# A three-pass float32r linear layer: steady weight tiles over four token blocks (256, 256, 256, 288) instead of three blocks of 352

## The chip, the cores and the metric

The kernel runs on one core of one Trainium2 chip. The metric is the device time of one launch in microseconds (us): the median of three runs before the change. Everything below comes from the reference, the kernel's text, these run times and the trace of one profiled execution.

## What is computed

One inference step of a two-layer trunk of width 1024. 1024 prompt tokens and 32 sample tokens (8 sequences of 4) share all weights, so each linear layer sees 1056 tokens. Layer 0 mixes tokens by a gated short convolution, layer 1 by stick-breaking attention; each is followed by a convolutional FFN of inner width 2816.

```python
h = rmsnorm(x, norm_mix[i])
if i % N_MIXERS == 0:                      # layer 0
    proj = h @ w_in                        # 1024 -> 3 * 1024
    b_gate, c_gate, v = split(proj, 3)
    y = (b_gate * causal_dwconv(c_gate * v, prev, w_dw)) @ w_out
else:                                      # layer 1
    qkv = h @ w_qkv
    y = stick_breaking(q, k, v, ...) @ w_o
x = x + y
h = rmsnorm(x, norm_ffn[i])
up = h @ w_up                              # 1024 -> 2 * 2816
g, u = split(up, 2)
a = silu(causal_dwconv(g, prev, w_dw) + b_dw) * u
x = x + a @ w_down                         # 2816 -> 1024
```

## The kernel before

**Numbers.** Activations and weights are float32. Each is split in two float32r parts, `hi` and `lo`, and a product is made of three passes of TensorE: `w_hi*hi`, `w_hi*lo` and `w_lo*hi`, all added up in PSUM. The helper `three` issues the three matmuls of one block; each has its own load of 128x128 weights in front. float32r and float32 both stand as "f32" in the rows of PE.

**Tiles.** All weights are cut into 196 tiles of 128x1024 (24 for `sc_in`, 8 for `sc_out`, 66 for each FFN, 24 for `qkv`, 8 for `wo`). A tile is brought in by a DMA into `raw`, split by POOL (w_hi L506, w_lo L508), and used 8 times 128 columns. Tokens are the moving side: 1056 = 3 blocks of TW = 352 columns, so a weight block of 128x128 gives 3 blocks x 3 passes = 9 matmuls, and a tile 72; 196 tiles give 14112.

**PSUM.** `out[0]` and `out[1]` have three banks of 512 float32 each. A block of 352 tokens stands at the start of each bank; `result(s)` is the view 128x3x352 over them. The two are used in turn: PE waits for `taken[s]`, fills, and raises `full[s]`; DVE (or ACT) then reads all 1056 columns in one instruction and raises `taken[s]`.

**Places.** `linear` (a whole tile, contraction over k inside) and `down` (the FFN's second product: two tiles are summed into each of 8 outputs) are the steady code. The first tile of a stage (`first_linear`, which waits for its input block by block), the last (`last_linear`), the last `down` of an FFN (`last_down`) and the attention's `project` work block by block with other semaphores. PE's program is written out in full and its order is that of the code; nothing is scheduled at run time.

**Readers of PSUM named below.** `ffn_chunk` (L1463 and L1474), `add_x` (L1486), the short convolution (L1525), and ACT's `copy_gate` (L958).

Of the kernel before, what the change touches and what calls it, by code (L numbers as in the profile page):

```python
# [27 lines left out]
T = SEQ + NS  # L28
TJ = 3
TW = T // TJ  # L30
F = 2816
FC = F // P
CW = 3
# [143 lines left out]
def build(nc, x_in, weights, taps_sc, taps_ffn, state_sc, state_ffn, gains, bias_heads, bias_rows,  # L177
# [6 lines left out]
    with ctx:  # L184
# [103 lines left out]
        def result(s):  # L288
            return out[s][:, :, 0:TW]

        score = [out[1][:, 0:2, :].rearrange("p a b -> p (a b)"), spare[:, :, :].rearrange("p a b -> p (a b)")]
        def wide(t):
            return t.rearrange("p (a b) -> p a b", a=TJ)
# [4 lines left out]
        def tokens(j):  # L298
            return slice(j * TW, (j + 1) * TW)

# [237 lines left out]

        @block.tensor
        def _(pe):  # L540
            def three(o, w, c0, hi, lo, first, last, counts=False):

                mm = nc.tensor.matmul(o, w_hi[w][:, c0:c0 + P], hi, start=first, stop=False)  # L543
                if counts:
                    mm.then_inc(w_used, 1)
                nc.tensor.matmul(o, w_hi[w][:, c0:c0 + P], lo, start=False, stop=False)  # L546
                return nc.tensor.matmul(o, w_lo[w][:, c0:c0 + P], hi, start=False, stop=last)  # L547

            def mean_of(nth, j, n):

# [12 lines left out]
            def linear(tile, ring, s, fill, midway=None):  # L563

                pe.wait_ge(w_split, tile + (RAW + 1))

                pe.wait_ge(taken[s], fill + 1)
                for k in range(KC):
                    for j in range(TJ):

                        mm = three(out[s][:, j, 0:TW], ring, k * P, h_hi[:, k, tokens(j)],
                                   h_lo[:, k, tokens(j)], k == 0, k == KC - 1, k == j == 0)
                    if midway is not None:
                        midway(k)
                mm.then_inc(full[s], 1)
# [51 lines left out]
            def down(tile, ring0, k0, name, trip, slot, group, early_release):  # L627

                order = [(f, kk) for f in range(KC) for kk in range(2)]
                if early_release:  # L630


                    order[-4:] = [(KC - 2, 0), (KC - 1, 0), (KC - 2, 1), (KC - 1, 1)]
                release = (KC - 2, 1) if early_release else (KC - 1, 1)
                for f, kk in order:
                    s = (k0 + f + 1) % 2
                    if f == 0:

                        pe.wait_ge(w_split, tile + (RAW + 1 + kk))
                        pe.wait_ge(a_ready, group * 2 + (3 + kk))  # L640
                    if kk == 0:
                        pe.wait_ge(taken[s], trip * TRIP_FILLS + (FREE[name][s] + (k0 + f) // 2 + 1))
                    for j in range(TJ):

                        mm = three(out[s][:, j, 0:TW], (ring0 + kk) % SPLIT, f * P,
                                   a_hi[:, slot, kk, j * TW:(j + 1) * TW],
                                   a_lo[:, slot, kk, j * TW:(j + 1) * TW], kk == 0, kk == 1,
                                   j == 0 and (f, kk) in (order[0], release))
                    if kk == 1:
                        mm.then_inc(full[s], 1)  # L650

# [304 lines left out]
        def _(act):  # L956
# [36 lines left out]
            def copy_gate(m):  # L993
                n, k = m % 2, 3 * m
                s = (k + 1) % 2
                act.wait_ge(convolved, m + 1)
                act.wait_ge(full[s], FULL["sc_in"][s] + k // 2 + 1)
                act_op(wide(c_gate[n][:, :]), result(s)).then_inc(taken[s], 1)

            def first_norm():  # L1000
                act.preload_act_table(ACT.Sqrt)
# [325 lines left out]
        def _(dve):  # L1327
# [52 lines left out]

            def norm_of_projection(nth, name, base):
                for f in range(KC - 1):
                    add_x(f, name, f, 0)
                    n = SUM_BASE[nth] + f
                    dve.wait_ge(squared, SQ_BASE[nth] + f + 1)
                    if f == 0:
                        V.tensor_copy(total[:, :], square[0][:, :]).then_inc(summed, 1)
                    else:
                        dve.wait_ge(summed, n)
                        V.tensor_tensor(total[:, :], total[:, :], square[f % 2][:, :], ALU.add).then_inc(summed, 1)  # L1390
                f, added = KC - 1, TJ * (nth // 2)
                s = (f + 1) % 2
                for j in range(TJ):
                    dve.wait_ge(block_full, base + j + 1)
                    V.tensor_tensor(x[:, f, tokens(j)], x[:, f, tokens(j)], out[s][:, j, 0:TW], ALU.add).then_inc(x_added, 1)
                    for g in range(KC):
                        low(nth, g, j)
                for j in range(TJ):
                    sum_block(nth, f, j, f + j)
                dve.wait_ge(x_added, added + TJ)  # L1400
                dve.sem_inc(taken[s], 1)
                invert_all(nth)
# [51 lines left out]
                        last.then_inc(tapped, 1)  # L1454
                last.then_inc(convolved, 1)

            def ffn_chunk(m, par, chunk, layer, k, trip, slot, between=None):
                name = f"ffn{layer}"
                s = (k + 1) % 2

                dve.wait_ge(convolved, m + 1)
                dve.wait_ge(full[s], trip * TRIP_FILLS + (FULL[name][s] + k // 2 + 1))
                V.tensor_tensor(wide(ext[par][:, CW - 1:]), result(s), wide(rstd[:, :]), ALU.mult).then_inc(taken[s], 1)  # L1463
                dve.wait_ge(taken[s], trip * TRIP_FILLS + (FREE[name][s] + k // 2 + 2))

                dve.wait_ge(a_ready, m - (KC - 1))
                conv(m, par, lambda t: tap_ffn[:, ds(chunk + layer * FC, 1), t:t + 1].rearrange("p o t -> p (o t)"))
                s = (k + 2) % 2
                dve.wait_ge(silued, m - (KC - 1))
                V.tensor_tensor(y[par][:, :], y[par][:, :], rstd[:, :], ALU.mult).then_inc(y_scaled, 1)  # L1470
                dve.wait_ge(y_scaled, m + 1)
                dve.wait_ge(full[s], trip * TRIP_FILLS + (FULL[name][s] + (k + 1) // 2 + 1))
                yy = wide(y[par][:, :])
                V.tensor_tensor(yy, yy, result(s), ALU.mult).then_inc(taken[s], 1)  # L1474
                if between is not None:
                    between()
                dve.wait_ge(a_high, m - (KC - 1))
                V.tensor_tensor(a_lo[:, slot, par, :], y[par][:, :], a_hi[:, slot, par, :].bitcast(f32),
                                ALU.subtract).then_inc(a_ready, 1)

            def add_x(f, name, k, trip):

                s = (k + 1) % 2
                dve.wait_ge(full[s], trip * TRIP_FILLS + (FULL[name][s] + k // 2 + 1))
                xx = x[:, f, :].rearrange("p (a b) -> p a b", a=TJ)
                V.tensor_tensor(xx, xx, result(s), ALU.add).then_inc(taken[s], 1)  # L1486

            def ffn(layer):
                name = f"ffn{layer}"
                m0 = M_FFN[layer]  # L1490

                def up(m, chunk, k0, trip, slot, between=None):
                    for p in range(2):
                        ffn_chunk(m + p, p, chunk + p, layer, k0 + 2 * p, trip, slot, between if p else None)

                def down(k0, trip):
                    for f in range(1, KC):
                        add_x(f, name, k0 + f, trip)

                up(m0, 0, 0, 0, 0)  # L1500
                with dve.Fori(0, FFN_TRIPS) as i:
                    for n in range(2):
                        k0 = (4 + KC) * n + 4
                        up(i * 4 + (m0 + 2 + 2 * n), i * 4 + (2 + 2 * n), k0, i, (n + 1) % 2,
                           lambda: add_x(0, name, k0 + 4, i))
                        down(k0 + 4, i)
# [7 lines left out]
            def sc_in_chunk(i, n, last=False):  # L1514
# [7 lines left out]
                V.tensor_tensor(c_gate[n][:, :], c_gate[n][:, :], rstd2[:, :], ALU.mult).then_inc(c_scaled, 1)  # L1522
                dve.wait_ge(c_scaled, m + 1)
                dve.wait_ge(full[s], i * 3 + (FULL["sc_in"][s] + k // 2 + 1))
                V.tensor_tensor(wide(ext[n][:, CW - 1:]), wide(c_gate[n][:, :]), result(s), ALU.mult).then_inc(taken[s], 1)  # L1525
                dve.wait_ge(taken[s], i * 3 + (FREE["sc_in"][s] + k // 2 + 2))
                conv(m, n, lambda t: tap_sc[:, ds(m, 1), t:t + 1].rearrange("p o t -> p (o t)"))

# [12 lines left out]
                    dve.sem_inc(taken[s], 1)  # L1541
                else:
                    dve.wait_ge(full[s], i * 3 + (FULL["sc_in"][s] + k // 2 + 1))
                    V.tensor_tensor(mixed[:, ds(m, 1), :].rearrange("p o (a b) -> p (o a) b", a=TJ),
                                    wide(y[n][:, :]), result(s), ALU.mult).then_inc(taken[s], 1)

            with dve.Fori(0, KC // 2 - 1) as i:
                for n in range(2):
# [250 lines left out]
```

## Time and profile before

| | |
|---|---|
| Runs | 2622.76 us median of 3 (2622.29 to 2626.1) |
| Profiled execution, first to last instruction (span) | 2615.1 us |
| PE (matmul) busy | 2570.0 us, 98% |
| PE weight load busy | 2443.8 us, 93% |
| DVE, ACT, POOL busy | 1374.5, 550.8, 708.4 us |
| Mean granted TensorE clock | 0.996 |

The profile gives the span of the profiled execution, and no other time of it; the median of the runs lies 7.7 us above that span, which is what lies around it. Busy time of PE counts each matmul from its start to its last result, and neighbours overlap, so a busy share near 100% says that PE hardly waits, and the distance from one start to the next says what a matmul costs.

### The profile page before, as it was taken

How to read it: one execution, taken by the hardware profiler on the slowest of the kernel's cores; microseconds unless marked ns; L12 is line 12 of the kernel's file. 1: busy time of each engine (PE TensorE's matmuls, PEld its weight loads, DVE VectorE, ACT ScalarE, POOL GpSimd, SP SyncE). 2: the span in 40 equal slices, each digit the busy share in tenths (PEclk: the TensorE clock that was granted, in tenths of full speed). 3: DMA queues.
4: the chain of work that ended last, by engine and by line, in shares of the span. 5: the costliest groups of instructions: out<-in, count | busy, mean ns of one | idle time of the engine just before them, and what ended most of it. 6: DMA issues, size and time to landing. Idle time of an engine off the chain costs nothing.

```text
span 2615.1 us, 40858 instructions
## 1 busy us (share of the span) xinstructions
PE 2570.0 (98%) x16982; PEld 2443.8 (93%) x16982; DVE 1374.5 (53%) x1346; ACT 550.8 (21%) x1145; POOL 708.4 (27%) x405
## 2 busy tenths in 40 slices
PE   8999999999999999999999999999999999999997
PEld 7999999999999999988888888669999999999996
DVE  5333446444544444476667666654644455444445
ACT  4000221000000000144444444542100000000012
POOL 3333333323322333322111111013332332233331
PEclk9999999999999999999999999999999999999999
DMA  4111111111111111122111111641111111111111
GB/s 142 43 47 49 47 44 49 41 49 48 42 41 49 49 49 49 44 70 95 35 40 36 39 42 42 211 172 41 49 41 49 49 41 41 49 49 49 49 44 67
DMA packets 62523, 149.06 MB, mean 57 GB/s; under 512 B 5666, under 2 KB 28962, under 8 KB 62370
## 3 DMA queue, kind: packets, MB, share of 16 engines
q1 hardware_dynamic: 56130, 130.35, 15.6%
q10 hardware_dynamic: 6240, 16.36, 1.6%
q8 instruction: 134, 2.20, 0.4%
q14 instruction: 19, 0.16, 0.0%
HBM read 128.91 MB, written 17.78 MB: 56 GB/s over the span
## 4 chain that ended last, share of the span: by engine, by line
PE 92%; DVE 5%; issue 2%; ACT 1%; POOL 1%; DMA 0%; DVEq 0%; POOLq 0%; ACTq 0%; SPq 0%
PE bank L543 28%; PE bank L547 28%; PE bank L546 27%; PE bank L807 2%; PE bank L745 2%; DVE prod L1591 2%; PE bank L778 2%; DVE beta L1595 1%; PE bank L680 0%; PE bank L748 0%; DVE h_lo L1432 0%; DVE rstd L1366 0%; PE bank L881 0%; PE bank L912 0%; POOL w_lo L521 0%
## 5 line engine op out<-in xcount | busy, mean ns | idle before, releaser
L543 PE MATMUL bank<-h_hi,w_hi 128*128 128x352 f32 x3648 | 1189.0, 326 | 14.4 <-DVE h_lo L1352 7.6
L547 PE MATMUL bank<-h_hi,w_lo 128*128 128x352 f32 x3648 | 1175.2, 322 | 0.0
L546 PE MATMUL bank<-h_lo,w_hi 128*128 128x352 f32 x3648 | 1171.6, 321 | 0.0
L506 POOL CAST w_hi<-raw 128x1024 fp32r<-128x1024 f32 x194 | 212.5, 1095 | 1841.9 <-PE bank L543 1795.2
L543 PEld LDWEIGHTS bank<-h_hi,w_hi 128*128 128x128 f32 x3648 | 685.0, 188 | 24.2 <-issue 14.8
L546 PEld LDWEIGHTS bank<-h_lo,w_hi 128*128 128x128 f32 x3648 | 689.0, 189 | 0.8
L547 PEld LDWEIGHTS bank<-h_hi,w_lo 128*128 128x128 f32 x3648 | 685.1, 188 | 0.0
L508 POOL TENSOR_TENSOR w_lo<-raw,w_hi 128x1024 fp32r<-128x1024 f32 x194 | 478.4, 2466 | 15.5
L1486 DVE TENSOR_TENSOR x<-x,bank 128x1056 f32<-128x1056 f32 x174 | 218.3, 1254 | 320.5 <-PE bank L547 318.6
L543 PE MATMUL bank<-a_hi,w_hi 128*128 128x352 f32 x1056 | 343.7, 325 | 2.3 <-POOL w_lo L508 2.3
L546 PE MATMUL bank<-a_lo,w_hi 128*128 128x352 f32 x1056 | 340.8, 323 | 0.0
L547 PE MATMUL bank<-a_hi,w_lo 128*128 128x352 f32 x1056 | 340.7, 323 | 0.0
L1591 DVE TENSOR_TENSOR_SCAN prod<-keep 128x895 f32<-128x895 f32 (+7 forms) x128 | 216.6, 1692 | 86.9 <-ACT keep L958 80.0
L1463 DVE TENSOR_TENSOR ext<-bank,rstd 128x1056 f32<-128x1056 f32 x44 | 55.4, 1258 | 339.9 <-PE bank L547 339.8
L958 ACT ACTIVATE smp<-ext 128x32 f32<-128x32 f32 x52 | 12.0, 231 | 939.1 <-DVE ext L1463 850.9
L543 PEld LDWEIGHTS bank<-a_hi,w_hi 128*128 128x128 f32 x1056 | 198.4, 188 | 10.3 <-DVE x L1407 3.4
L546 PEld LDWEIGHTS bank<-a_lo,w_hi 128*128 128x128 f32 x1056 | 198.5, 188 | 0.3
L547 PEld LDWEIGHTS bank<-a_hi,w_lo 128*128 128x128 f32 x1056 | 198.4, 188 | 0.0
L1438 DVE TENSOR_SCALAR y<-ext,tap_ffn 128x1024 f32<-128x1024 f32 x44 | 116.5, 2649 | 9.7 <-DVE ext L1463 9.6
L958 ACT ACTIVATE beta<-bank,bias_pair 128x896 f32<-128x896 f32 (+7 forms) x128 | 94.9, 742 | 126.0 <-PE bank L748 120.7
L1445 DVE SCALAR_TENSOR_TENSOR y<-ext,tap_ffn,y 128x1024 f32<-128x1024 f32 x88 | 113.0, 1284 | 0.0
L1595 DVE TENSOR_TENSOR beta<-beta,prod 128x895 f32<-128x895 f32 (+7 forms) x128 | 106.2, 829 | 4.4
(129 smaller groups left out, 1622.3 us busy)
## 6 DMA issues: line engine op xcount, KB each, us to landing
raw<-weights SPq DMA_DIRECT2D x196, 512.0 KB, 3.5
x_spill<-x ACTq DMA_DIRECT2D x8, 528.0 KB, 5.1
k_out<-k_t ACTq DMA_DIRECT2D x8, 528.0 KB, 3.1
v_out<-v_t ACTq DMA_DIRECT2D x8, 528.0 KB, 2.7
x<-x_spill SPq DMA_DIRECT2D x8, 528.0 KB, 7.3
pages_hi<-cache_k SPq DMA_DIRECT2D x8, 512.0 KB, 6.0
pages_hi<-cache_v SPq DMA_DIRECT2D x8, 512.0 KB, 7.2
pages_lo<-cache_k SPq DMA_DIRECT2D x8, 512.0 KB, 7.4
```

The source lines that it names most:

```text
L506: nc.gpsimd.tensor_copy(w_hi[ring][:, :], raw[slot][:, :]).then_inc(w_high, 1)
L508: nc.gpsimd.tensor_tensor(w_lo[ring][:, :], raw[slot][:, :], w_hi[ring][:, :].bitcast(f32), ALU.subtract).then_inc(w_split, 1)
L543: mm = nc.tensor.matmul(o, w_hi[w][:, c0:c0 + P], hi, start=first, stop=False)
L546: nc.tensor.matmul(o, w_hi[w][:, c0:c0 + P], lo, start=False, stop=False)
L547: return nc.tensor.matmul(o, w_lo[w][:, c0:c0 + P], hi, start=False, stop=last)
L958: return nc.scalar.activation(o, i, func, **kw)
L1438: V.tensor_scalar(o[:, 0:SEQ], e[:, 0:SEQ], tap(0), None, ALU.mult).then_inc(tapped, 1)
L1445: main = V.scalar_tensor_tensor(o[:, 0:SEQ], e[:, n:n + SEQ], tap(n), o[:, 0:SEQ], ALU.mult, ALU.add)
L1463: V.tensor_tensor(wide(ext[par][:, CW - 1:]), result(s), wide(rstd[:, :]), ALU.mult).then_inc(taken[s], 1)
L1486: V.tensor_tensor(xx, xx, result(s), ALU.add).then_inc(taken[s], 1)
L1591: V.tensor_tensor_scan(prod[:, width - 1:0:-1], back, back, 1.0, ALU.mult, ALU.bypass).then_inc(scanned, 1)
L1595: V.tensor_tensor(w[:, 0:width - 1], w[:, 0:width - 1], prod[:, 1:width], ALU.mult).then_inc(weighed, 1)
```

## The change

In `linear` and `down` the 1056 tokens are cut at 256, 512 and 768. The output is no longer one block per bank: it stands contiguous from column 256 of the first bank to column 288 of the third (`flat(s)`), so that the first block fills the upper half of bank 0, the second and third fill bank 1, and the fourth, of 288, starts bank 2. Only the first block in each bank has the flag that clears (`CLEARS`). Readers of these tiles take one contiguous run of 1056 columns instead of three of 352. Tiles of `first_linear`, `last_linear`, `last_down` and `project` keep 352, and their readers keep `result(s)` (`by_blocks`).

```diff
+FLAT_AT = 256
+PARTS = ((0, 256), (256, 512), (512, 768), (768, T))
+CLEARS = (0, 256, 768)
+        def flat(s):
+            return out[s][:, :, :].rearrange("p a b -> p (a b)")[:, FLAT_AT:FLAT_AT + T]
...
                 for k in range(KC):
-                    for j in range(TJ):
-
-                        mm = three(out[s][:, j, 0:TW], ring, k * P, h_hi[:, k, tokens(j)],
-                                   h_lo[:, k, tokens(j)], k == 0, k == KC - 1, k == j == 0)
+                    for a, b in PARTS:
+
+                        mm = three(flat(s)[:, a:b], ring, k * P, h_hi[:, k, a:b], h_lo[:, k, a:b],
+                                   k == 0 and a in CLEARS, k == KC - 1, k == a == 0, True)
...
-                    for j in range(TJ):
-
-                        mm = three(out[s][:, j, 0:TW], (ring0 + kk) % SPLIT, f * P,
-                                   a_hi[:, slot, kk, j * TW:(j + 1) * TW],
-                                   a_lo[:, slot, kk, j * TW:(j + 1) * TW], kk == 0, kk == 1,
-                                   j == 0 and (f, kk) in (order[0], release))
+                    for a, b in PARTS:
+
+                        mm = three(flat(s)[:, a:b], (ring0 + kk) % SPLIT, f * P, a_hi[:, slot, kk, a:b],
+                                   a_lo[:, slot, kk, a:b], kk == 0 and a in CLEARS, kk == 1,
+                                   a == 0 and (f, kk) in (order[0], release), True)
...
+                if by_blocks:
+                    V.tensor_tensor(wide(ext[par][:, CW - 1:]), result(s), wide(rstd[:, :]), ALU.mult).then_inc(taken[s], 1)
+                else:
+                    V.tensor_tensor(ext[par][:, CW - 1:], flat(s), rstd[:, :], ALU.mult).then_inc(taken[s], 1)
```

On PE, at the start of the second tile of the program (a `linear` of the short convolution's input), one 128x128 block of weights is this before the change (`w_hi_55` and `w_lo_58` are the two parts of the tile):

```order
L543 MATMUL bank<-h_hi,w_hi_55 128x352
L546 MATMUL bank<-h_lo,w_hi_55 128x352
L547 MATMUL bank<-h_hi,w_lo_58 128x352
L543 MATMUL bank<-h_hi,w_hi_55 128x352
L546 MATMUL bank<-h_lo,w_hi_55 128x352
L547 MATMUL bank<-h_hi,w_lo_58 128x352
L543 MATMUL bank<-h_hi,w_hi_55 128x352
L546 MATMUL bank<-h_lo,w_hi_55 128x352
L547 MATMUL bank<-h_hi,w_lo_58 128x352
```

and this in the changed kernel:

```order
L552 MATMUL bank<-h_hi,w_hi_55 128x256
L555 MATMUL bank<-h_lo,w_hi_55 128x256
L556 MATMUL bank<-h_hi,w_lo_58 128x256
L552 MATMUL bank<-h_hi,w_hi_55 128x256
L555 MATMUL bank<-h_lo,w_hi_55 128x256
L556 MATMUL bank<-h_hi,w_lo_58 128x256
L552 MATMUL bank<-h_hi,w_hi_55 128x256
L555 MATMUL bank<-h_lo,w_hi_55 128x256
L556 MATMUL bank<-h_hi,w_lo_58 128x256
L552 MATMUL bank<-h_hi,w_hi_55 128x288
L555 MATMUL bank<-h_lo,w_hi_55 128x288
L556 MATMUL bank<-h_hi,w_lo_58 128x288
```

Nine matmuls became twelve, over the same 3 x 1056 columns. The whole program of PE has 11520 matmuls of 352 columns fewer, 11520 of 256 and 3840 of 288 more, and 2592 of its three-pass matmuls stay at 352. The other place is where the last `linear` of an FFN trip ends and `down` begins (`a_hi`, `a_lo` are the activated inner values). In the changed kernel, with the semaphores that the row waits for:

```order
L552 MATMUL bank<-h_hi,w_hi_54 128x288
L555 MATMUL bank<-h_lo,w_hi_54 128x288
L556 MATMUL bank<-h_hi,w_lo_57 128x288
L552 MATMUL bank<-a_hi,w_hi_55 128x256 [waits taken1,a_ready,w_split]
L555 MATMUL bank<-a_lo,w_hi_55 128x256
```

Before the change the same five rows are of 352 columns, with the same waits at the same row. No instruction of DVE, ACT, POOL or SP is added or taken away; those that read PSUM have another access pattern of the same 1056 columns.

## Rows read from the trace of the kernel before

**Rows 1.** The page: busy time, slices, the chain by line, costliest groups.

```profile
PE 2570.0 (98%) x16982; PEld 2443.8 (93%) x16982; DVE 1374.5 (53%) x1346; ACT 550.8 (21%) x1145; POOL 708.4 (27%) x405
...
PEclk9999999999999999999999999999999999999999
...
PE bank L543 28%; PE bank L547 28%; PE bank L546 27%; PE bank L807 2%; PE bank L745 2%; DVE prod L1591 2%; PE bank L778 2%; DVE beta L1595 1%; PE bank L680 0%; PE bank L748 0%; DVE h_lo L1432 0%; DVE rstd L1366 0%; PE bank L881 0%; PE bank L912 0%; POOL w_lo L521 0%
...
L543 PE MATMUL bank<-h_hi,w_hi 128*128 128x352 f32 x3648 | 1189.0, 326 | 14.4 <-DVE h_lo L1352 7.6
```

**Rows 2.** PE in time order, steady tile: start us, us, instruction.

```profile
1000.09 0.32 PE L543 MATMUL bank<-h_hi,w_hi 128*128 128x352 f32 x1
1000.25 0.32 PE L546 MATMUL bank<-h_lo,w_hi 128*128 128x352 f32 x1
...
1003.93 0.32 PE L543 MATMUL bank<-h_hi,w_hi 128*128 128x352 f32 x1
```

**Rows 3.** Windows: from:to length, busy (x count), then granted clock, DMA share, GB/s.

```profile
100.00:280.00 180.00, 180.00 (x1135) 180.00 (x1134) 56.03 (x51) 8.99 (x26) 61.01 (x32) 1.00 0.15 45
500.00:1000.00 500.00, 500.00 (x3113) 498.17 (x3112) 233.94 (x199) 40.83 (x98) 150.98 (x88) 1.00 0.15 47
```

**Rows 4.** Other forms on PE in time order, same columns as rows 2.

```profile
400.31 1.05 PE L552 MATMUL bank<-total,mean 128*128 128x352 f32 x3
...
1208.69 0.87 PE L778 MATMUL bank<-ident,beta 128*128 128x128 f32 x6
...
1208.69 1.09 PE L778 MATMUL bank<-ident,beta 128*128 128x128 f32 x8
...
1211.21 0.28 PE L748 MATMUL bank<-diag_b,ident_b 128*128 128x128 bf16 x2
1211.42 0.99 PE L807 MATMUL bank<-w_second,v_rows 128*64 128x128 f32 x14
```

**Rows 5.** By line: duration ns min/median/max of those forms.

```profile
L552 PE MATMUL bank<-total,mean x12: 456/458/460, 400.3 to 1844.0; 128*128 128x352 f32 x12
...
L748 PE MATMUL bank<-diag_b,ident_b x128: 218/224/231, 1192.2 to 1720.1; 128*128 128x128 bf16 x128
```

**Rows 6.** Weight loads by line; then in time order, after a stop and steady.

```profile
L680 PEld LDWEIGHTS bank<-square,mean x72: 105/107/110, 25.4 to 2598.2; 128*32 128x32 f32 x72
...
L552 PEld LDWEIGHTS bank<-total,mean x12: 187/189/189, 400.1 to 1843.7; 128*128 128x128 f32 x12
...
L778 PEld LDWEIGHTS bank<-ident,beta x576: 137/140/145, 1205.6 to 1727.3; 128*128 128x128 f32 x192
...
55.84 0.19 PEld L543 LDWEIGHTS bank<-h_hi,w_hi 128*128 128x128 f32 x1 [1.93 <-issue]
55.94 0.19 PEld L546 LDWEIGHTS bank<-h_lo,w_hi 128*128 128x128 f32 x1
...
1000.25 0.19 PEld L547 LDWEIGHTS bank<-h_hi,w_lo 128*128 128x128 f32 x1
```

**Rows 7.** PE waits, longest first: us in total, times, longest us.

```profile
PE bank L543 <- DVE h_lo L1352: 7.6, 2, 7.4
...
PE bank L543 <- DVE ext L1525: 1.7, 1, 1.7
```

**Rows 8.** DVE by line and form: busy us, mean ns, idle before, releaser.

```profile
L1486 DVE TENSOR_TENSOR x<-x,bank 128x1056 f32<-128x1056 f32 x174 | 218.3, 1254 | 320.5 <-PE bank L547 318.6 <-DMA x<-x_spill 2.0
...
L1470 DVE TENSOR_TENSOR y<-y,rstd 128x1056 f32<-128x1056 f32 x44 | 57.3, 1303 | 55.1 <-ACT y L958 55.1
```

**Rows 9.** PE in time order, first steady stage.

```profile
150.01 0.32 PE L546 MATMUL bank<-h_lo,w_hi 128*128 128x352 f32 x1
150.16 0.32 PE L547 MATMUL bank<-h_hi,w_lo 128*128 128x352 f32 x1
...
150.48 0.32 PE L546 MATMUL bank<-h_lo,w_hi 128*128 128x352 f32 x1
150.65 0.32 PE L547 MATMUL bank<-h_hi,w_lo 128*128 128x352 f32 x1
```

More of the change, by code:

```diff
@@ L540, in _, with three @@
         def _(pe):
-            def three(o, w, c0, hi, lo, first, last, counts=False):
-                mm = nc.tensor.matmul(o, w_hi[w][:, c0:c0 + P], hi, start=first, stop=False)
+            def three(o, w, c0, hi, lo, first, last, counts=False, shared=False):
+                mm = nc.tensor.matmul(o, w_hi[w][:, c0:c0 + P], hi, start=first, stop=False, skip_group_check=shared)
                 if counts:
                     mm.then_inc(w_used, 1)
-                nc.tensor.matmul(o, w_hi[w][:, c0:c0 + P], lo, start=False, stop=False)
-                return nc.tensor.matmul(o, w_lo[w][:, c0:c0 + P], hi, start=False, stop=last)
+                nc.tensor.matmul(o, w_hi[w][:, c0:c0 + P], lo, start=False, stop=False, skip_group_check=shared)
+                return nc.tensor.matmul(o, w_lo[w][:, c0:c0 + P], hi, start=False, stop=last, skip_group_check=shared)
             def mean_of(nth, j, n):
@@ L997, in copy_gate @@
                 act.wait_ge(full[s], FULL["sc_in"][s] + k // 2 + 1)
-                act_op(wide(c_gate[n][:, :]), result(s)).then_inc(taken[s], 1)
+                if m == 0:
+                    act_op(wide(c_gate[n][:, :]), result(s)).then_inc(taken[s], 1)
+                else:
+                    act_op(c_gate[n][:, :], flat(s)).then_inc(taken[s], 1)
             def first_norm():
@@ L1382, in norm_of_projection @@
                 for f in range(KC - 1):
-                    add_x(f, name, f, 0)
+                    add_x(f, name, f, 0, f == 0)
                     n = SUM_BASE[nth] + f
@@ L1455, in conv, with ffn_chunk @@
                 last.then_inc(convolved, 1)
-            def ffn_chunk(m, par, chunk, layer, k, trip, slot, between=None):
+            def ffn_chunk(m, par, chunk, layer, k, trip, slot, between=None, by_blocks=False):
                 name = f"ffn{layer}"
@@ L1462, in ffn_chunk @@
                 dve.wait_ge(full[s], trip * TRIP_FILLS + (FULL[name][s] + k // 2 + 1))
-                V.tensor_tensor(wide(ext[par][:, CW - 1:]), result(s), wide(rstd[:, :]), ALU.mult).then_inc(taken[s], 1)
+                if by_blocks:
+                    V.tensor_tensor(wide(ext[par][:, CW - 1:]), result(s), wide(rstd[:, :]), ALU.mult).then_inc(taken[s], 1)
+                else:
+                    V.tensor_tensor(ext[par][:, CW - 1:], flat(s), rstd[:, :], ALU.mult).then_inc(taken[s], 1)
                 dve.wait_ge(taken[s], trip * TRIP_FILLS + (FREE[name][s] + k // 2 + 2))
@@ L1472, in ffn_chunk @@
                 dve.wait_ge(full[s], trip * TRIP_FILLS + (FULL[name][s] + (k + 1) // 2 + 1))
-                yy = wide(y[par][:, :])
-                V.tensor_tensor(yy, yy, result(s), ALU.mult).then_inc(taken[s], 1)
+                V.tensor_tensor(y[par][:, :], y[par][:, :], flat(s), ALU.mult).then_inc(taken[s], 1)
                 if between is not None:
@@ L1479, in ffn_chunk, with add_x @@
                                 ALU.subtract).then_inc(a_ready, 1)
-            def add_x(f, name, k, trip):
+            def add_x(f, name, k, trip, by_blocks=False):
                 s = (k + 1) % 2
                 dve.wait_ge(full[s], trip * TRIP_FILLS + (FULL[name][s] + k // 2 + 1))
-                xx = x[:, f, :].rearrange("p (a b) -> p a b", a=TJ)
-                V.tensor_tensor(xx, xx, result(s), ALU.add).then_inc(taken[s], 1)
+                if by_blocks:
+                    V.tensor_tensor(wide(x[:, f, :]), wide(x[:, f, :]), result(s), ALU.add).then_inc(taken[s], 1)
+                else:
+                    V.tensor_tensor(x[:, f, :], x[:, f, :], flat(s), ALU.add).then_inc(taken[s], 1)
             def ffn(layer):
@@ L1490, in ffn, with up @@
                 m0 = M_FFN[layer]
-                def up(m, chunk, k0, trip, slot, between=None):
+                def up(m, chunk, k0, trip, slot, between=None, first=False):
                     for p in range(2):
-                        ffn_chunk(m + p, p, chunk + p, layer, k0 + 2 * p, trip, slot, between if p else None)
+                        ffn_chunk(m + p, p, chunk + p, layer, k0 + 2 * p, trip, slot, between if p else None, first and p == 0)
                 def down(k0, trip):
@@ L1498, in down @@
                         add_x(f, name, k0 + f, trip)
-                up(m0, 0, 0, 0, 0)
+                up(m0, 0, 0, 0, 0, first=True)
                 with dve.Fori(0, FFN_TRIPS) as i:
@@ L1524, in sc_in_chunk @@
                 dve.wait_ge(full[s], i * 3 + (FULL["sc_in"][s] + k // 2 + 1))
-                V.tensor_tensor(wide(ext[n][:, CW - 1:]), wide(c_gate[n][:, :]), result(s), ALU.mult).then_inc(taken[s], 1)
+                V.tensor_tensor(ext[n][:, CW - 1:], c_gate[n][:, :], flat(s), ALU.mult).then_inc(taken[s], 1)
                 dve.wait_ge(taken[s], i * 3 + (FREE["sc_in"][s] + k // 2 + 2))
@@ L1543, in sc_in_chunk @@
                     dve.wait_ge(full[s], i * 3 + (FULL["sc_in"][s] + k // 2 + 1))
-                    V.tensor_tensor(mixed[:, ds(m, 1), :].rearrange("p o (a b) -> p (o a) b", a=TJ),
-                                    wide(y[n][:, :]), result(s), ALU.mult).then_inc(taken[s], 1)
+                    V.tensor_tensor(mixed[:, ds(m, 1), :].rearrange("p o t -> p (o t)"),
+                                    y[n][:, :], flat(s), ALU.mult).then_inc(taken[s], 1)
             with dve.Fori(0, KC // 2 - 1) as i:
```

## Prediction

> **What bounds the kernel now.** I read the page first: PE is busy 98% of the span, the clock row is at its upper level (2.4 GHz) throughout, and in the chain that ended last the three lines of the three-pass product, L543, L546 and L547, hold 28 + 27 + 28 = 83% [rows 1]. So time is won or lost in how fast these matmuls follow each other. Next PE's waits: the longest single one is 7.4 us at the start, and no entry is of a steady tile that waits for its PSUM buffer for more than the single 1.7 us stop [rows 7]. PE streams.
>
> The busy time of one matmul, 326 ns [rows 1], is its whole way through the array, and neighbours overlap. What one costs is the distance of starts. In time order these are 0.16 us apart; 24 of them lie between the starts at 1000.09 and 1003.93, so 3.84 us / 24 = 160.0 ns each [rows 2]. Over long stretches, taking off the two in flight at the edge, it is 180/1133 = 158.9 ns while POOL and DVE are rather quiet and 500/3111 = 160.7 ns in the FFN [rows 3]. I take 160.0.
>
> At 2.4 GHz, 352 columns take 146.7 ns, so **a matmul costs 13.3 ns more than its columns** (12.2 to 14.0 by the two stretches). What this excess is made of decides the whole prediction, so I looked at what other forms have. Three float32 matmuls of 352 columns at L552 take 1.05 us, of which the last's own 0.458: 0.592/2 = 296 ns apart [rows 4, 5], which is 352 columns at half the rate (293.3) and 2.7. Transposes of 128 columns: eight end 0.22 us after six, 110 ns each [rows 4], that is 106.7 at half the rate and 3. Two bf16 matmuls at L748, at the full rate: 280 - 224 = 56 ns [rows 4, 5], 53.3 and 2.7. So every other form has an excess of about 3, and only float32r, 4 bytes per column at full rate, has 13. That it moves from place to place (starts 0.15 to 0.17 us apart in one stretch, [rows 9]) makes it look like the way operands are fetched.
>
> **The change, part by part.** (1) Matmuls. Of the 14112 three-pass matmuls 11520 lie in `linear` and `down`; they are 3840 groups of one pass over 1056 columns. Three become four, with the same columns. So the columns cost nothing more (1056/2.4 = 440.0 ns per group either way) and what changes is the excess: now 3 x 13.3 = 40 per group. If it is paid per matmul, the group goes from 480.0 to 440.0 + 4 x 13.3 = 493.3 ns, and 3840 x 13.3 = **+51.1 us**. With 12.2 and 14.0 for the excess: +47 and +54.
>
> Why per matmul: the three other forms, with 352 and 128 columns at either rate, all have the same 3 ns, so there the excess doesn't grow with the columns; and the variation of the float32r one by place is of a few ns per instruction. Why perhaps not: there is one width of float32r in this trace, and no row can separate a share per column from a share per matmul. That is the step I trust least.
>
> The Trainium skill (TensorE: Matmul & The Clock Gate, "Back-to-back issue gap") gives N/2.4 + 2.5 ns for warm matmuls. The rows of L552, L778 and L748 agree with it; the 160 ns of the float32r rows do not (it would give 149.2). By this rule an added matmul costs 2.5 ns and the change 3840 x 2.5 = +9.6 us; that is close to the second rival below.
>
> (2) Weight loads. Each added matmul has its own load, and all loads now have less to hide behind: 256 columns last 106.7 ns. A load of 32 columns shows 107 ns, one of 128 columns 189 [rows 6]: 82 ns for 96 columns, 0.85 ns each, so 109 ns of pure loading for 128. After a stop the second load starts 0.10 us after the first, when the first matmul begins [rows 6]: the same number. A load starts when the matmul before begins (both at 1000.25, [rows 2, 6]), so a block can't be shorter than about 110 ns; with the excess it is 120. I cost the loads at nothing. The cover shrinks from 50 ns to 10: if it fails, each nanosecond of a block costs 15.4 us over 15360 blocks. That is the third rival.
>
> (3) Reading instructions: 7680 more on PE, in pairs each 120 ns. In the attention 14 matmuls of L807 with their loads pass in 0.99 us [rows 4], less than 71 ns a pair. At nothing.
>
> (4) Readers of PSUM. DVE takes 1254 ns for 1056 columns out of three banks in three runs, and 1303 ns for 1056 contiguous ones in SBUF [rows 8]: no sign that three runs cost anything. Nobody waits for them either: a tile takes 72 x 160 = 11.5 us and an output of `down` 18 x 160 = 2.9 us, against 1.25 of DVE, which waited 318.6 us for PE there [rows 8]. If a reader were 0.1 us longer, it would still end before the other buffer is full. Below nothing: where PE stops for DVE's L1525 (1.7 us, once, [rows 7]) a faster reader gives back at most some tenths. At nothing.
>
> (5) Stages that keep 352 (2592 matmuls, the attention, the norms) are as before. POOL delivers w_hi and w_lo per tile as before, and has more time.
>
> Sum against the profiled execution: 2615.1 + 51.1 = 2666.2 us of span. The runs' median lies 7.7 above that span, so 2622.8 + 51.1 = **2673.9**; I say 2673.
>
> **The rivals.**
>
> *Excess per column.* Say only 3 ns (what the other forms have; 2.7 by L748) are per matmul and the remaining 10.6 ns belong to the 352 columns, as if 4 bytes per column could not quite be fetched at full rate. Then a column costs 157.3/352 = 0.447 ns, 256 cost 117.1, 288 cost 131.4, the group 482.7: 2.7 x 3840 = +10.4, **2633**. If all of it is per column: no change, 2623. For it: full-rate columns of 2 bytes and half-rate columns of 4 bytes show no excess, only full-rate 4 bytes does, which is what a limit of the fetch would look like. Against: the starts vary by place, 0.15 to 0.17.
>
> *Blocks are fetched in units, and 256 fits them (faster).* 160.0 ns is exactly 384 columns, the next multiple of 64 (and of 128) over 352. If a block costs its columns rounded up to 64, then 256 columns cost 106.7, held at about 110 by the weight load, and 288 cost 320/2.4 = 133.3. The group is 3 x 110 + 133.3 = 463.3 ns instead of 480.0, 3840 x 16.7 = -64 us, **2559**. It decides as soon as a 256-column matmul takes less than 115 ns (at 288 with 133). For it: the exact 160.0 in the middle of the stretches, and blocks that now start at multiples of 1024 bytes from each other, where 352 columns are 1408 bytes. Against: 158.9 on average over 180 us, and starts 0.15 apart, are under 160, which a strict rounding would not allow; L552 with its 352 columns shows none. With a unit of 128 columns, 288 would cost 160 and the group 490: +38 us, like my forecast.
>
> *The weight load shows.* If the excess comes on top of whichever is longer, load or columns, a 256 block costs 110 + 13.3 = 123.3, the 288 block 133.3, the group 503.3: 3840 x 23.3 = +89 us, **2712**. For it: the margin is 10 ns, and nothing in this trace has a 128x128 float32 load under a full-rate matmul as short as 107 ns (the transposes' loads take 140 ns instead of 189 [rows 6], L748's are bf16). Against: the load starts with the matmul before, and 109 fit in 120.
>
> The Trainium skill says of loads (same page, "LDWEIGHTS") that one takes columns/1.2, 107 ns for 128. The rows agree (109); by it alone the load stays hidden and this rival falls away.
>
> *The change does not do what it says* is no case: the order of the rows shows the four blocks in all 3840 groups.
>
> **How the numbers follow.** Excess per matmul 0.42 (time 2673, its own range 2649 to 2698: excess of 11.7 to 14.9 ns on a block, as places differ by a few ns); per column 0.16 (2620 to 2640, of which 0.06 lie within 0.2%); units of 64 0.32 (2545 to 2615); load shows 0.10 (2700 to 2730). 0.2% is 5 us, about what a measurement can tell from no change. Faster 0.32 plus 0.01 of the second case, same 0.06, slower 0.61. The likeliest single case gives the time; the range must take in the units' case, since leaving it out would lose three in ten: from 2552 to 2702 it leaves out about 0.13.
>
> **What the trace after would show.** Starts of 256-column matmuls 120 ns apart and of the 288-column one 133: forecast. 117 and 131: per column. 110 and 133: units. 123 and more, with the weight load's start as late as the matmul's: load. PE's share stays at 98%, and DVE's readers stay near 1254 ns. I would be wrong outside of all this if waits for `taken` appeared in the steady tiles, if DVE's contiguous reads got much slower, or if the granted clock fell.

## The result, and the profile after

| | before | after |
|---|---|---|
| Median of the runs, us | 2622.76 | 2646.79 (2646.79 to 2648.14) |
| Ratio, 95% interval | | 1.0096 (1.0076 to 1.0115) |
| Span of the profiled execution, us | 2615.1 | 2646.4 |
| Clock granted to TensorE, mean | 0.996 | 0.995 |

The changed kernel is 24 us slower; 2673 was forecast, inside a range of 2552 to 2702. The sign was right and the size of the added cost was half of what I gave.

The page of the changed kernel, against [rows 1]:

```profile
PE 2598.7 (98%) x20822; PEld 2473.0 (93%) x20822; DVE 1375.3 (52%) x1346; ACT 551.0 (21%) x1145; POOL 700.9 (26%) x405
...
PEclk9999999999999999999999999999999999999999
...
PE bank L552 28%; PE bank L555 28%; PE bank L556 27%; PE bank L815 2%; PE bank L753 2%; DVE prod L1606 2%; PE bank L786 2%; DVE h_lo L1363 1%; DVE beta L1610 1%; PE bank L756 0%; PE bank L688 0%; DVE h_lo L1443 0%; DVE rstd L1377 0%; PE bank L920 0%; PE bank L889 0%
```

3840 more matmuls, the same 98% and the same 83% of the chain: PE still streams, and what changed is its pace. In time order (start us, us, instruction), in a steady tile:

```profile
1000.46 0.28 PE L552 MATMUL bank<-a_hi,w_hi 128*128 128x256 f32 x1
1000.58 0.28 PE L555 MATMUL bank<-a_lo,w_hi 128*128 128x256 f32 x1
1000.69 0.28 PE L556 MATMUL bank<-a_hi,w_lo 128*128 128x256 f32 x1
...
1001.52 0.30 PE L552 MATMUL bank<-a_hi,w_hi 128*128 128x288 f32 x1
1001.65 0.29 PE L555 MATMUL bank<-a_lo,w_hi 128*128 128x288 f32 x1
1001.78 0.30 PE L556 MATMUL bank<-a_hi,w_lo 128*128 128x288 f32 x1
1001.91 0.28 PE L552 MATMUL bank<-a_hi,w_hi 128*128 128x256 f32 x1
```

Nine matmuls of 256 columns lie between 1000.46 and 1001.52, 117.8 ns each; three of 288 take 0.39 us, 130. Over all of the trace the mean distance of starts is 117.8 ns for 256 columns, 133.4 for 288 and, in the kernel before, 159.9 for 352 (stops and the gaps of missing records left out). Less the columns at 2.4 GHz, the excess is 11.1, 13.4 and 13.2 ns. The windows of [rows 3], now:

```profile
100.00:280.00 180.00, 180.00 (x1479) 180.00 (x1478) 54.44 (x50) 7.96 (x25) 55.92 (x30) 1.00 0.14 48
500.00:1000.00 500.00, 500.00 (x4105) 499.03 (x4104) 233.65 (x201) 40.87 (x98) 143.64 (x84) 1.00 0.14 46
```

Taking off the two in flight, both are 121.9 ns per matmul: 487.5 per group of four, where three of before took 476.7 in the first stretch and 482.1 in the second. So a group costs 5 to 11 ns more. From the means, 3 x 117.8 + 133.4 = 486.8 against 479.6, and 3840 x 7.1 = 27 us. That is the change, within the 20 to 30 us of the interval.

The cost is not spread evenly. Four groups of a `linear` tile (operands `h_hi`, `h_lo`) and three of `down` (`a_hi`, `a_lo`), each row being the first matmul of a weight block:

```profile
150.12 0.28 PE L552 MATMUL bank<-h_hi,w_hi 128*128 128x256 f32 x1
...
155.97 0.28 PE L552 MATMUL bank<-h_hi,w_hi 128*128 128x256 f32 x1
...
1000.46 0.28 PE L552 MATMUL bank<-a_hi,w_hi 128*128 128x256 f32 x1
...
1004.81 0.28 PE L552 MATMUL bank<-a_hi,w_hi 128*128 128x256 f32 x1
```

The first pair spans four weight blocks, 5.85 us / 12 = 487.5 ns per group of one pass; the second spans three, 4.35 us / 9 = 483.3. Over all of the trace `linear` has 118.0 and 133.7 ns for its two widths, a group of 487.8 where it had 479.5 before, and `down` has 117.1 and 132.3, 483.5 where it had 480.1. So 2880 groups of `linear` carry some 24 us and 960 of `down` some 3. In `linear` the three blocks of 256 are 116.7, 119.7 and 117.7 ns long, in `down` 116.7, 117.3 and 117.2: the cost of one width depends on what is read.

Readers and waits show nothing:

```profile
L1501 DVE TENSOR_TENSOR x<-x,bank 128x1056 f32<-128x1056 f32 x172 | 215.7, 1254 | 324.1 <-PE bank L556 324.1
...
PE bank L552 <- DVE ext L1540: 1.5, 1, 1.5
```

1254 ns for the contiguous 1056 columns, exactly as in [rows 8], and a stop of 1.5 us for the 1.7 of [rows 7]. The longest sum of waits went from 7.6 to 11.1 us, at norms whose code is not changed. The traces of experiments 1, 3 and 6, whose layers are those of the kernel before, have 10.7 to 10.9 us there, so it differs between executions of one kernel and is not an effect of the change; all of PE's waits together went only from 34.8 to 36.8 us.

The two spans differ by 31.3 us and the medians by 24, because the profiled execution of the kernel before was a short one. All later runs lie 1.7 to 1.8 us above their own span, not 7.7, and the kernel before takes from 2616.4 to 2629.5 us in them. The 7.7 us between its median and its span are mostly this spread, and not time around the span.

### The profile page after: what moved, and what is told of

It reads as the page before. It is cut to its first block, busy times and chain, and to the rows that moved or that the text cites. A ratio compares the mean times of both kernels' runs of the same rounds, so it can differ in the third digit from the quotient of the medians.

```text
span 2646.4 us, 48538 instructions
## 1 busy us (share of the span) xinstructions
PE 2598.7 (98%) x20822; PEld 2473.0 (93%) x20822; DVE 1375.3 (52%) x1346; ACT 551.0 (21%) x1145; POOL 700.9 (26%) x405
## 3 DMA queue, kind: packets, MB, share of 16 engines
q1 hardware_dynamic: 56130, 130.35, 14.7%
## 4 chain that ended last, share of the span: by engine, by line
PE 92%; DVE 6%; issue 1%; ACT 1%; POOL 0%; DMA 0%; DVEq 0%; ACTq 0%; POOLq 0%
PE bank L552 28%; PE bank L555 28%; PE bank L556 27%; PE bank L815 2%; PE bank L753 2%; DVE prod L1606 2%; PE bank L786 2%; DVE h_lo L1363 1%; DVE beta L1610 1%; PE bank L756 0%; PE bank L688 0%; DVE h_lo L1443 0%; DVE rstd L1377 0%; PE bank L920 0%; PE bank L889 0%
## 5 line engine op out<-in xcount | busy, mean ns | idle before, releaser
L552 PE MATMUL bank<-h_hi,w_hi 128*128 128x256 f32 (+2 forms) x4608 | 1354.8, 294 | 16.8 <-DVE h_lo L1363 11.1
L555 PE MATMUL bank<-h_lo,w_hi 128*128 128x256 f32 (+2 forms) x4608 | 1341.1, 291 | 0.0
L556 PE MATMUL bank<-h_hi,w_lo 128*128 128x256 f32 (+2 forms) x4608 | 1336.9, 290 | 0.0
L552 PEld LDWEIGHTS bank<-h_hi,w_hi 128*128 128x128 f32 x4608 | 869.5, 189 | 26.8 <-issue 13.9
L555 PEld LDWEIGHTS bank<-h_lo,w_hi 128*128 128x128 f32 x4608 | 868.7, 189 | 0.8
L556 PEld LDWEIGHTS bank<-h_hi,w_lo 128*128 128x128 f32 x4608 | 867.9, 188 | 0.0
L552 PE MATMUL bank<-a_hi,w_hi 128*128 128x256 f32 (+1 forms) x1376 | 396.0, 288 | 2.3 <-POOL w_lo L517 2.3
L555 PE MATMUL bank<-a_lo,w_hi 128*128 128x256 f32 (+1 forms) x1376 | 394.0, 286 | 0.0
L556 PE MATMUL bank<-a_hi,w_lo 128*128 128x256 f32 (+1 forms) x1376 | 393.5, 286 | 0.0
L1501 DVE TENSOR_TENSOR x<-x,bank 128x1056 f32<-128x1056 f32 x172 | 215.7, 1254 | 324.1 <-PE bank L556 324.1
L552 PEld LDWEIGHTS bank<-a_hi,w_hi 128*128 128x128 f32 x1376 | 258.5, 188 | 9.5 <-DVE x L1418 3.4
L555 PEld LDWEIGHTS bank<-a_lo,w_hi 128*128 128x128 f32 x1376 | 258.7, 188 | 0.3
```

The source lines that it names most:

```text
L1501: V.tensor_tensor(x[:, f, :], x[:, f, :], flat(s), ALU.add).then_inc(taken[s], 1)
```

## Experiments

**1. The width by itself.** The step that I trusted least was that the excess belongs to the matmul and not to its columns. One width cannot tell, so I put a bench behind the kernel's end.

```diff
+            pe.wait_ge(y_made, sum(Y_BY_DVE))
+            pe.wait_ge(y_by_pool, sum(Y_BY_POOL))
+            for count, at_col, n in ((60, 0, 512), (40, 0, 64), (40, 0, 128), ..., (40, 16, 256), (40, 32, 256), ...):
+                for _ in range(count):
+                    nc.tensor.matmul(out[0][:, 0, 0:n], w_hi[0][:, 0:P], a_hi[:, 0, 0, at_col:at_col + n],
+                                     start=True, stop=True, skip_group_check=True)
```

> The kernel before, with matmuls added behind its end, when every other engine has finished its work on chip: one float32r weight block and moving columns from one place, 40 times each for widths of 64 to 512 columns, then 256, 288 and 352 columns from starts that are shifted by 16 to 96 columns. The added time is a bench and no part of the computation. Theory of a cost per matmul (13 ns over the columns): 512 columns are 226 ns apart, 288 are 133, 256 are 120, 192 stop at the weight load's 110. Theory of a cost per column (2.7 ns and 0.0301 ns per column): 512 are 231 ns apart, 256 117, 352 160. Theory of units of 64 columns: steps in the widths, 320 and 304 cost the same, 512 costs 213 to 216. If the place decides, the shifted starts differ from the unshifted by several ns; else by none. The weight load alone: 64, 128 and 192 columns all at about 110.

Mean distance of starts in ns (the first two distances of a case left out), and the excess over n/2.4:

| columns | 256 | 272 | 288 | 304 | 320 | 352 | 384 | 416 | 448 | 480 | 512 |
|---|---|---|---|---|---|---|---|---|---|---|---|
| distance | 116.7 | 125.7 | 133.3 | 140.1 | 146.6 | 160.0 | 173.3 | 186.7 | 206.6 | 220.0 | 233.3 |
| excess | 10.0 | 12.4 | 13.3 | 13.4 | 13.3 | 13.3 | 13.3 | 13.4 | 19.9 | 20.0 | 20.0 |

None of my three theories. The excess is 13.3 over a wide range, as a cost per matmul would have it, then jumps to 20.0. From 256 to 512 the excess doubles with the columns (0.039 ns per column at both), and between them it moves in uneven steps. There are no steps of 64 columns: 304 is between 288 and 320. Shifted starts changed 256 columns by up to 3 ns (117.8 to 120.1 for shifts of 16 to 96 columns), 352 by up to 2. 64 columns were 112 ns apart, at the upper clock. The cases of 128 and 192 columns ran in part at the lower clock and are measured again in experiment 3.

**2. Three blocks, contiguous.** It undoes the fourth matmul and keeps the readers.

```diff
-PARTS = ((0, 256), (256, 512), (512, 768), (768, T))
+PARTS = ((0, 256), (256, 768), (768, T))
```

> The changed kernel with the second and third block joined: 256, 512 and 288 columns, three matmuls for each weight block and pass as in the kernel before, with the contiguous readers of the changed one. By the trace of the changed kernel, 256 columns are 117.9 ns apart and 288 are 133.5. Theory of a cost per matmul of 13 ns: 512 takes 226, the group 477.8 against 479.7 before, 3840 groups -7 us, so 2615 or the same as before. Theory of a cost that grows with the columns: 512 takes 231 to 236, the group 482 to 487, 2632 to 2651. If the readers' contiguous pattern cost something, the time would be above what the matmuls give.

Measured: 2633.87 us, ratio to the kernel before 1.0043 (1.0027 to 1.0058). Three matmuls again, and still 11 us slower than before. Its trace has 118.3, 232.5 and 132.6 ns for 256, 512 and 288 columns, the group 483.4: the excess of 512 columns is 19.1, and 3840 x 3.8 = +15 us. Its window, to be set against [rows 3]:

```profile
500.00:1000.00 500.00, 500.00 (x3090) 452.09 (x3089) 233.52 (x200) 40.85 (x98) 144.12 (x84) 1.00 0.14 45
```

500/3088 is 161.9 ns per matmul, 485.8 per group, where the kernel before has 482.1. A fixed cost of 13.3 ns per matmul is refuted: it allowed 226 ns and no loss. In these kernels the fourth matmul itself cost the other half, 487 - 483 ns.

**3. Forms and widths, each on a line.**

```diff
+            for _ in range(16): nc.tensor.matmul(out[0][:, 0, 0:128], w_hi[0][:, 0:P], a_hi[:, 0, 0, 0:128], ...)
+            for _ in range(40): nc.tensor.matmul(out[0][:, 0, 0:512], ...)
...
+            for _ in range(30): nc.tensor.matmul(..., w_hi[0][:, 0:P].bitcast(bf16)[:, 0:P], a_hi[...].bitcast(bf16)[:, 0:512], ...)
+            for _ in range(30): nc.tensor.matmul(out[0][0:32, 0, 0:352], w_hi[0][:, 0:32], a_hi[:, 0, 0, 0:352], ...)
...
+            walk(((0, 256), (256, 512), (512, 768), (768, T)), ((0, 256), (1, 0), (1, 256), (2, 0)))
```

> The kernel before with a second bench behind its end (added time, no part of the computation), each case on its own line: 128 and 192 columns with TensorE kept at its upper clock by 512-column blocks in between; float32r widths of 224 to 464; bf16 of 512 and 352 columns; 352 float32r columns with 128, 64 and 32 columns of weights; and the three passes walking over the tokens as the kernels do, cut 352/352/352, 256/256/256/288, 256/512/288, 400/400/256 and 384/416/256. The first bench showed an excess over the columns of 10 ns at 256, 13.3 from 288 to 416 and 20.0 from 448 to 512. Theory of stops at fixed stretches of a float32r stream: a step of 6.7 ns near 430 columns and none between 288 and 420, bf16 shows 3 ns or less at 512, and the number of weight columns changes nothing. Theory that the weight load takes the time from the matmul: 64 and 32 columns of weights have clearly less excess than 13.3. Loads alone: 128 and 192 columns both about 109 to 112. The walks, per pass over 1056 columns: 480.0, 487, 483.5, 478 and 478.

PE in time order; one row is a whole case of so many matmuls:

```profile
2632.84 1.90 PE L958 MATMUL bank<-a_hi,w_hi 128*128 128x128 f32 x16
...
2643.95 1.93 PE L960 MATMUL bank<-a_hi,w_hi 128*128 128x192 f32 x16
...
2665.24 3.67 PE L965 MATMUL bank<-a_hi,w_hi 128*128 128x256 f32 x30
...
2686.79 5.76 PE L970 MATMUL bank<-a_hi,w_hi 128*128 128x416 f32 x30
...
2698.14 6.06 PE L972 MATMUL bank<-a_hi,w_hi 128*128 128x432 f32 x30
...
2722.51 6.65 PE L976 MATMUL bank<-a_hi,w_hi 128*128 128x512 bf16 x30
...
2743.08 4.96 PE L980 MATMUL bank<-a_hi,w_hi 128*32 128x352 f32 x30
2747.88 4.96 PE L981 MATMUL bank<-a_hi,w_hi 128*128 128x352 f32 x30
```

and, by line, the mean duration of one (last number in front of the idle time), which is to be taken off a row's total before it is divided by the count less one:

```profile
L976 PE MATMUL bank<-a_hi,w_hi 128*128 128x512 bf16 x30 | 6.6, 379 | 0.0
...
L980 PE MATMUL bank<-a_hi,w_hi 128*32 128x352 f32 x30 | 5.0, 322 | 0.0
...
L965 PE MATMUL bank<-a_hi,w_hi 128*128 128x256 f32 x30 | 3.7, 280 | 0.0
```

256 columns: (3.67 - 0.28)/29 = 116.9 ns. bf16 of 512: (6.65 - 0.379)/29 = 216.2, excess 2.9, where float32r has 20 (experiment 1). Weights of 32 columns (L980) give the row of 128 (L981): 160.0 both. So the weight load has no part in it at 352 columns; at 256, nearer the floor, it was not tried. The step near 430 is there but not sharp: 13.3 at 416, 15.3 at 424, 16.6 at 432, 17.8 at 448 and 464. At 448 experiment 1 had 19.9, from the same start; why two executions differ by 2 ns there is open. Below 240 the load binds: 128, 192 and 224 columns are all 112 ns apart once a case's first distances are left out (with them, L958: (1.90 - 0.27)/15 = 109).

The walks, per pass over 1056 tokens, by mean distances of starts: 352/352/352 480.0; 256/256/256/288 483.6; 256/512/288 483.4; 400/400/256 482.1; 384/416/256 478.8. I had expected 480.0, 487, 483.5, 478 and 478: the second and fourth are misses. The last is the only cut that came out below three blocks of 352; no kernel was run with it. Four blocks cost 3.6 ns here and 7.1 in the kernel, and here they cost no more than 256/512/288. The walks read `a_hi` and `a_lo`, and `down`, which reads the same in the changed kernel, has 483.5 as well, with a new weight block for each group and sums kept in PSUM. So the rest lies in `linear` alone, with 487.8. No bench read `h_hi` or `h_lo`, so whether their place in memory makes it is not shown.

**4. The floor of the load, in the kernel.**

```diff
+PARTS = ((0, 256), (256, 512), (512, 768), (768, 912), (912, T))
```

> The changed kernel with its last block of 288 cut in two of 144 columns: five blocks. By columns and an excess of 13 ns two blocks of 144 cost 146 ns; by the weight load's floor of 109 to 112 they cost 218 to 224 in place of 133. With the floor: 3840 groups x 85 to 91 ns = +326 to +349 us against the changed kernel, 2975 to 3000; without it +50 us, about 2697.

Measured 2999.1 us, in a single run. The starts of its 144-column matmuls:

```profile
1000.03 0.28 PE L552 MATMUL bank<-a_hi,w_hi 128*128 128x144 f32 x1
1000.14 0.27 PE L555 MATMUL bank<-a_lo,w_hi 128*128 128x144 f32 x1
1000.25 0.27 PE L556 MATMUL bank<-a_hi,w_lo 128*128 128x144 f32 x1
```

110 ns apart for 60 ns of columns, and +352 us over the four blocks: the floor that I had from the loads' durations is real, and 256 columns stand 6 to 8 ns above it.

**5. Blocks of 400, 400 and 256.** Experiment 1 has 13.3 at 384 and at 416 columns, so 400 should have it too, and 256 has 10 to 11. A kernel that could beat both.

```diff
+PARTS = ((0, 400), (400, 800), (800, T))
+        def placed(s, a, b):
+            return out[s][:, a // 400, 0:b - a]
...
-                V.tensor_tensor(x[:, f, :], x[:, f, :], flat(s), ALU.add).then_inc(taken[s], 1)
+                by_two(s, lambda q, o: V.tensor_tensor(o, o, q, ALU.add), lambda a, b: x[:, f, a:b])
```

> Three blocks of 400, 400 and 256 columns, each at the start of its bank, and readers of PSUM in two instructions (2 x 400, then 256) in place of one. If an excess is 13.3 ns for any width up to 416 and 11.5 for 256, the group costs 440.0 + 38.2 = 478.2 ns against 479.6 before: 3840 x -1.4 = -5 us, about 2617. If the excess is per column, the group stays at 480 and the time at 2623. If the second reading instruction matters, slower than before.

Measured 2628.52 us, ratio 1.0023 (1.0012 to 1.0033): slower than before, a miss. 400 columns took 182.6 ns in the kernel (182.1 in the walk), an excess of 16.0 and not the 13.3 of a block that is read again and again from one place; 256 took 117.1. Group 482.3, 3840 x 2.7 = +10 us, a little over the 3 to 9 us of the interval. The second reading instruction is not seen: DVE takes 988 + 414 ns in place of 1254, and PE's waits are as before.

**6. What is read.** 512 columns throughout.

```diff
+            for _ in range(30): nc.tensor.matmul(..., a_hi[:, 0, 0, 0:1].broadcast_to([P, 512]), ...)
+            for _ in range(30): nc.tensor.matmul(..., a_hi[:, 0, 0, 0:1024].rearrange('p (a b) -> p a b', b=2)[:, :, 0], ...)
+            for _ in range(30): nc.tensor.matmul(..., a_hi[...].bitcast(bf16).rearrange('p (a b) -> p a b', b=2)[:, :, 0], ...)
```

> The kernel before with a bench behind its end (added time, no part of the computation): 512 columns each, 30 times. The cases: float32r from one run of bytes; float32r that reads the same single column 512 times; float32r with every second column; bf16 from one run; bf16 with every second element (so 4 bytes of step); float32r on 64 and on 32 partitions. Plain float32r has an excess of 20 ns, bf16 2.5. Theory that the excess is in fetching 4 bytes per column from memory: the single column has 3 ns or little, and the spaced bf16, which passes over as many bytes as float32r, has up to 20. Theory that it belongs to the float32r format inside the array: all float32r cases have 20, also the single column, and both bf16 cases 2.5. Fewer partitions change nothing by either theory.

```profile
2630.55 7.16 PE L958 MATMUL bank<-a_hi,w_hi 128*128 128x512 f32 x30
2637.56 6.72 PE L959 MATMUL bank<-a_hi,w_hi 128*128 128x512 f32 x30
2644.11 13.76 PE L960 MATMUL bank<-a_hi,w_hi 128*128 128x512 f32 x30
2657.70 6.67 PE L961 MATMUL bank<-a_hi,w_hi 128*128 128x512 bf16 x30
2664.21 6.95 PE L962 MATMUL bank<-a_hi,w_hi 128*128 128x512 bf16 x30
2671.09 7.26 PE L963 MATMUL bank<-a_hi,w_hi 64*128 64x512 f32 x30
```

The mean distances over the columns' 213.3 ns, the first two of each case left out, are: float32r in one run (L958) 20.0; the same column each time (L959) 5.3; every second column (L960) 240; bf16 in one run (L961) 2.5; bf16 with a 4-byte step (L962) 13.2; float32r on 64 partitions (L963) 20.0. How the moving side goes through memory makes most of the excess: float32r without moving on loses 14.7 of its 20 ns, and bf16 that passes over as many bytes as float32r gains 10.7 of the 17.5 that part them. The theory that all of it belongs to the format inside the array is out. Whether it is the bytes passed over or the step between columns that costs bf16 its 10.7 is not separated: a step costs float32r much more (L960). The Trainium skill (SBUF — State Buffer, "Specifications (TRN2)") says that each crossing to a new 16-byte line pays a penalty, and that two hits per line are needed for full bandwidth. L958 against L959 agrees in kind. The rest does not: bf16 in one run crosses as many lines with 512 columns as float32r with 256, and has an excess of 2.5 and not 10; and L960, with two hits per line, ran at half the rate. The case of 32 partitions ran at the lower clock and tells nothing here.

**7. The change in the whole tiles alone.** `down` and its readers go back to 352.

```diff
-                    for a, b in PARTS:
+                    for j in range(TJ):
...
-                        add_x(f, name, k0 + f, trip)
+                        add_x(f, name, k0 + f, trip, True)
```

> The changed kernel with the four blocks in the whole-tile code alone; the FFN's second product and its readers are again as before, with 352. 2880 of the 3840 groups are changed. If the cost is in the matmuls alone (7.1 ns a group by the changed kernel's trace, 24 to 27 us in all), three quarters of it stay: +18 to +20 us against the kernel before, 2641 to 2644. If instead a wait between DVE and PE in the FFN's second product carried a part of it, more than a quarter would go: nearer 2630.

Measured 2642.22 us, ratio 1.0066 (1.0053 to 1.0080): +17.5 us with 2880 of the 3840 groups, near three quarters of the cost. The interval, 14 to 21 us, is too wide to divide the cost more closely; it lies below the 24 us that the changed kernel's trace gives `linear`, and the trace of this run has the same 118.0 and 133.7 ns there. That gap is open. A wait in `down` with a large part of its own is excluded: most of the cost stays without it.

## Why the prediction was right or wrong

- **What bounds the kernel.** Right. The three lines hold 83% of the chain after, PE is at 98%, and the spacing of matmuls accounts for the change.
- **(1) Matmuls: "3 x 13.3 = 40 per group. If it is paid per matmul, ... +51.1 us."** The count was right and so was the way: a group cut in four costs more. The size of the term was not; this is the step that failed, and the one that was named as least trusted. An added matmul cost 7.1 ns and not 13.3, since 256 columns have an excess of 11.1: the excess grows with the columns, if in uneven steps (0.039 ns per column at 256 and at 512). Strictly per column the group would not have changed. What is left is that 352 columns come out low on those steps (0.0375 ns per column in the kernel) and 256 and 288 high (0.043 and 0.047), most of all in `linear`, for a reason that stays open.
- **The range.** 2647 lies between the own ranges of two cases, 2620 to 2640 for the excess per column and 2649 to 2698 for the excess per matmul. It is inside 2552 to 2702 because that had been drawn wide for a third case, the units of 64, which is refuted. That much is luck.
- **The argument for it** was wrong in kind: I took three forms that have no such excess (float32 at half rate, transposes, bf16) as evidence on how the one form that has it would scale. Experiment 3 has bf16 at 2.5 to 2.9 ns for 352 and 512 columns, so the form lacks the cost at any width that was tried; the other two were not run again. Where the Trainium skill's N/2.4 + 2.5 ns (TensorE: Matmul & The Clock Gate, "Back-to-back issue gap") is said to agree with L552 and L778, only the 2.5 does, since their rows show both at half the rate (296 ns for 352 columns, 110 for 128). The rival near its +9.6 us is the first of the list, not the second.
- **Rival, excess per column** (2633, chance 0.16): nearest of all in its numbers. It gave 117.1 ns for 256 columns (measured 117.8), 131.4 for 288 (133.4), and for 512, which its figures 2.7 + 0.0301 per column make 231.5, the kernel of experiment 2 has 232.5. The result lies 14 us above it, which is 3.6 ns per group; the trace makes it 4.1, 288 columns 2.0 too dear and three of 256 0.7 each.
- **Rival, units of 64 columns** (2559, chance 0.32): refuted by experiment 1. The exact 160.0 is no multiple of a unit: 352 columns show 13.3 ns from any start but one, and 304 and 320 differ by 6.5 ns. I had given it too much.
- **Rival, the weight load shows** (2712): refuted. The floor is at 109 to 112 ns as worked out, 256 columns stand above it, and the excess does not come on top of a load (experiments 3 and 4).
- **(2) loads, (3) instructions, (4) readers, (5) other stages at nothing:** right. Readers take 1254 ns as before, and two reading instructions in place of one cost nothing that is seen (experiment 5).

## What to carry to other kernels

To find whether a cost belongs to an instruction or to its columns, a trace with one width says nothing, and forms that lack the cost say no more: run a second width, which is one line of code. Where TensorE streams float32r at its full rate, count some 9% over the columns (13.3 on 146.7 ns, 20.0 on 213.3), for any of the cuts tried here, and never go below the columns that cover the weight load (here 240). A wider block is not cheaper by itself: 512 columns have more excess per column than 352, and the kernel with 256/512/288 was slower than that with three blocks of 352. A cut that looks best when one block is read again and again must be tried while walking over the tokens: 400 columns lost 2.7 ns on that way.

## What the runs showed of the hardware that was not expected

- float32r at 2.4 GHz has an excess that grows in uneven steps: 10.0 ns over 256 columns, 13.3 from 288 to 416, 20.0 at 480 and 512, and values between at 272 and from 424 to 464.
- Before the clock's first rise, which the trace has at 11.8 us, the same instruction is 0.29 us apart for 352 columns in the kernel before, which is 352/1.2 = 293 ns and no excess; behind it the distance is 0.16 us. The trace has no record of the clock ahead of that rise, so that it was the lower one is read from the distances.
- Blocks of one width, 256, differ in `linear` by what they read: 114.6 to 121.2 ns by block and pass, each the same to 0.1 ns in the trace of experiment 7.
- A step of 8 bytes between float32r columns halves the rate (453 ns for 512), one of 4 bytes costs bf16 10.7 ns, reading one column again costs 5.3 over the columns.
- Matmuls of 512 columns on 32 partitions, back to back, were followed by a fall of the granted clock to 1.2 GHz while PE was never idle. This was seen in one trace, and that the few partitions caused it is not shown. The stretches (from:to length, busy, granted clock, DMA) are of 64 partitions, 32 partitions twice, and 128 partitions:

```profile
2671.00:2678.00 7.00, 7.00 (x31) 1.00 0.00 0
2678.30:2682.00 3.70, 3.70 (x15) 0.89 0.00 0
2683.00:2688.00 5.00, 5.00 (x13) 0.50 0.00 0
...
2695.00:2698.50 3.50, 3.50 (x17) 1.00 0.00 0
```
